# Delta recurrence: the output's state products right behind the w products, its attention products behind the state products

## The chip, the core and the metric

The kernel runs on one core of one Trainium2 chip. The metric is the device time in microseconds (us) of one execution; lower is better. Three executions of the kernel before took 5368.41, 5379.1 and 5381.07 us; their median, 5379.1, is the time that a changed kernel is compared with.

## The reference

The program is one inference step of a two-layer hybrid decoder (1024 prompt tokens and 8 sample tokens), in fp32. Only one of its stages is touched here: the chunked gated delta rule of the second layer, for the prompt. Its 8 heads have keys and values of 128 columns. Time is cut into chunks of C = 64 tokens, and a state `s` (128x128 for each head) is carried from chunk to chunk:

```python
def step(s, inp):
    q_i, k_i, u_i, w_i, g_i, a_i = inp
    v_new = u_i - jnp.einsum('bhck,bhkv->bhcv', w_i, s)
    o = (jnp.einsum('bhck,bhkv->bhcv', q_i * jnp.exp(g_i)[..., None], s)
         + jnp.einsum('bhij,bhjv->bhiv', a_i, v_new))
    g_last = g_i[..., -1:]
    s = (s * jnp.exp(g_last)[..., None]
         + jnp.einsum('bhck,bhcv->bhkv', k_i * jnp.exp(g_last - g_i)[..., None], v_new))
    return s, o
```

So `v_new` needs the old state, the new state needs `v_new`, and the output `o` is a sum of two products: one of the old state (the state part) and one of `v_new` (the attention part). Nothing in the recurrence needs `o`.

## The kernel before

The program is a row of stages, each a block of its own with one instruction list for each engine. `delta_phase` is the stage of the recurrence. It loops over NPAIR = 8 pairs of chunks. For each pair it first prepares both chunks at once (norms, gates, Gram products, and five levels of a triangular solve, whose result is `xt`), and then takes the two chunks, p = 0 and p = 1, one after the other through the recurrence, since the second needs the first one's state. This last part is the one that is changed. The eight heads are one instruction each on TensorE, and one instruction for all heads on the other engines. For each chunk, in the order in which the parts depend on each other:

- **w products** (line 2129): TensorE, keys (`kbe`) times state `st_`, into banks 0 and 1.
- **r0** (line 2244): VectorE, `bv` minus the w products. TensorE waits for it (`r_ready`).
- **u products** (line 2134): TensorE, `xt` times r0, into banks 2 and 3.
- **vn** (line 2177): ScalarE copies them to `vn`, the new values. TensorE waits for it (`u_copied`). VectorE meanwhile scales the old state into `tmp` (line 2249).
- **state products** (line 2139): TensorE, `ktm` times `vn`, into banks 6 and 7.
- **output products** (lines 2141 and 2143): TensorE, for each head the state part (`st_` times `qe`) and then the attention part (`vn` times `at`), which accumulate in banks 4 and 5.
- **S** (line 2252): VectorE, `tmp` plus the state products, is the new state. It waits for `s_done`, which the last output product raises. TensorE's next w products wait for S (`s_ready`).

After p = 1, ScalarE copies the output of both chunks out of PSUM (line 2180, which also waits for `s_done`) and the norm of the output follows. An fp32 matmul of the program is two records in the trace, so eight heads are 16. The order of work on each engine is the order of the code; waits on semaphores are the only other rule. The profile shows `r0` as `dn_r`, `at` as `dn_mat`, `st_` as `dn_S` and `xt` as `dn_mxt`, and PSUM as `ps`.

Of the kernel before, what the change touches and what calls it, by code (L numbers as in the profile page):

```python
# [42 lines left out]
C = 64  # L43
# [1986 lines left out]
def delta_phase(T, ba):  # L2030
# [4 lines left out]
    nc, h, ps, io = T.nc, T.h, T.ps, T.io  # L2035
    sems = Sems(nc, "dn")
    S = {n: sems(n) for n in (
        "rows_in", "z_in", "squared", "sq_sum", "rn_log", "rn", "ba_cut", "spread", "l_copied", "l_exp", "unit", "turned", "k_copied",
        "ba_turned", "tm_ready", "kd_ready", "diff", "diff_exp", "keyed", "gram", "blocks_copied", "blocks_ready", "xm_ready", "xt_ready", "zt_done",
        "y_done", "y_ready", "z_done", "solved", "masked", "w_done", "r_ready", "u_done", "u_copied", "s_done", "s_ready",  # L2040
        "o_copied", "o_sq", "o_sum", "rs_log", "rs", "out_ready", "step", "cleared", "pe_passed", "end_diff", "end_exp",
        "state_out")}
    ones, ident, sel = T.const("ones"), T.const("ident"), T.const("sel")
    W = 2 * C
    with ExitStack() as ctx:
# [4 lines left out]
        Lb, eL, kb, kbe, qe, ktm, bv, r0, vn, st_, tmp, o, rs = (sb("_" + n, [P, 8, W]) for n in  # L2050
                                                              "Lb eL kb kbe qe ktm bv r0 vn S tmp o rs".split())
# [6 lines left out]
        bank = lambda b, hd: b + hd // 4  # L2058
        col = lambda hd, a=0, n=W: slice((hd % 4) * W + a, (hd % 4) * W + a + n)
# [27 lines left out]
        @block.tensor  # L2087
        def _(pe):
            with pe.Fori(0, NPAIR) as i:
                pe.wait_ge(S["squared"], i + 1)  # L2090
                for b in range(4):
                    mm = pe.matmul(ps[:, b, :], ones, qk[:, 4 * b:4 * b + 4, :], start=True, stop=True)
                mm.then_inc(S["sq_sum"], 1)
                pe.wait_ge(S["ba_cut"], i + 1)
                for b, r in ((4, slice(A_ROW, A_ROW + 8)), (6, slice(BETA_ROW, BETA_ROW + 8))):
                    for hd in range(8):
                        mm = pe.matmul(ps[:, bank(b, hd), col(hd)], sel[r, hd * P:(hd + 1) * P], bs[r, :], start=True, stop=True)
                mm.then_inc(S["spread"], 1)
                pe.wait_ge(S["unit"], i + 1)
                for b, src in ((0, qk[:, 8:16, :]), (2, X[:, 16:24, :])):  # L2100
                    for hd in range(8):
                        mm = pe.transpose(ps[:, bank(b, hd), col(hd)], src[:, hd, :], ident)
                pe.wait_ge(S["l_copied"], i + 1)
                mm = pe.transpose(ps[:, 4, 0:P], bs[:, :], ident)
                mm.then_inc(S["turned"], 1)
                pe.wait_ge(S["keyed"], i + 1)

                def gram(b, left, right):
                    for hd in range(8):
                        for p in range(2):  # L2110
                            c = slice(C * p, C * p + C)
                            mm = pe.matmul(ps[64 * p:64 * p + 64, b, hc(hd)], left(hd)[:, c], right(hd)[:, c], start=True,
                                           stop=True)
                    mm.then_inc(S["gram"], 1)

                k_, q_, kb_ = (lambda hd: qk[:, 8 + hd, :]), (lambda hd: qk[:, hd, :]), (lambda hd: kb[:, hd, :])
                gram(5, k_, kb_)
                gram(6, kb_, k_)
                gram(7, k_, q_)
                pe.wait_ge(S["tm_ready"], i + 1)  # L2120
                solve_levels_pe(pe, T, S, i, mtl, xm, xt, y, (0, 1, 2), S["pe_passed"])
                pe.wait_ge(S["masked"], i + 1)
                pe.wait_ge(S["solved"], i + 1)
                for p in range(2):
                    r, a = slice(64 * p, 64 * p + 64), C * p
                    c = slice(a, a + C)
                    pe.wait_ge(S["s_ready"], 2 * i + p + 1)
                    for hd in range(8):
                        mm = pe.matmul(ps[r, bank(0, hd), col(hd)], kbe[:, hd, c], st_[:, hd, :], start=True, stop=True)
                    mm.then_inc(S["w_done"], 1)  # L2130
                    pe.wait_ge(S["r_ready"], 2 * i + p + 1)
                    alone(pe, S["pe_passed"])
                    for hd in range(8):
                        mm = pe.matmul(ps[r, bank(2, hd), col(hd)], xt[r, hc(hd)], r0[r, hd, :], start=True, stop=True)
                    mm.then_inc(S["u_done"], 1)
                    pe.wait_ge(S["u_copied"], 2 * i + p + 1)
                    alone(pe, S["pe_passed"])
                    for hd in range(8):
                        pe.matmul(ps[:, bank(6, hd), col(hd)], ktm[r, hd, :], vn[r, hd, :], start=True, stop=True)
                    for hd in range(8):  # L2140
                        pe.matmul(ps[:, bank(4, hd), col(hd, a, C)], st_[:, hd, :], qe[:, hd, c], start=True, stop=False,
                                  skip_group_check=True)
                        mm = pe.matmul(ps[:, bank(4, hd), col(hd, a, C)], vn[r, hd, :], at[r, hc(hd)], start=False, stop=True,
                                       skip_group_check=True)
                    mm.then_inc(S["s_done"], 1)
                pe.wait_ge(S["o_sq"], i + 1)
                for b in range(2):
                    mm = pe.matmul(ps[:, b, :], ones, rs[:, 4 * b:4 * b + 4, :], start=True, stop=True)
                mm.then_inc(S["o_sum"], 1)

        @block.scalar
        def _(act):
            act.preload_act_table_set(EXP_LN_SET)
            with act.Fori(0, NPAIR) as i:
                act.wait_ge(S["rows_in"], 16 * i + 16)
                act.activation(qk[:, :, :], X[:, 0:16, :], ACT.Square).then_inc(S["squared"], 1)
                act.wait_ge(S["sq_sum"], i + 1)
                act.activation(qk[:, :, :], ps[:, 0:4, :].rearrange("p b (h w) -> p (b h) w", h=4), ACT.Ln,
                               bias=T.vec("eps_rms")).then_inc(S["rn_log"], 1)
                act.wait_ge(S["rn_log"], i + 1)  # L2160
                act.activation(qk[:, :, :], qk[:, :, :], ACT.Exp, scale=-0.5).then_inc(S["rn"], 1)
                act.wait_ge(S["spread"], i + 1)
                act.activation(Lb[:, :, :], two(4), ACT.Copy).then_inc(S["l_copied"], 1)
                act.wait_ge(S["l_copied"], i + 1)
                act.activation(eL[:, :, :], Lb[:, :, :], ACT.Exp).then_inc(S["l_exp"], 1)
                act.wait_ge(S["turned"], i + 1)
                act.activation(bt[:, :], ps[:, 4, 0:P], ACT.Copy).then_inc(S["ba_turned"], 1)
                act.wait_ge(S["end_diff"], i + 1)
                act.activation(ek[:, :], ek[:, :], ACT.Exp).then_inc(S["end_exp"], 1)
                act.wait_ge(S["diff"], i + 1)  # L2170
                act.activation(dt_[:, :], dt_[:, :], ACT.Exp)
                act.activation(dn[:, :], dn[:, :], ACT.Exp).then_inc(S["diff_exp"], 1)
                solve_levels_act(act, T, S, i, y, (0, 1, 2))
                for p in range(2):
                    r = slice(64 * p, 64 * p + 64)
                    act.wait_ge(S["u_done"], 2 * i + p + 1)
                    act.activation(vn[r, :, :], ps[r, 2:4, :].rearrange("p b (h w) -> p (b h) w", h=4), ACT.Copy)\
                       .then_inc(S["u_copied"], 1)
                act.wait_ge(S["s_done"], 2 * i + 2)
                act.activation(o[:, :, :], two(4), ACT.Copy).then_inc(S["o_copied"], 1)  # L2180
                act.wait_ge(S["o_copied"], i + 1)
                act.activation(rs[:, :, :], o[:, :, :], ACT.Square).then_inc(S["o_sq"], 1)
                act.wait_ge(S["o_sum"], i + 1)
                act.activation(rs[:, :, :], two(0), ACT.Ln, scale=1.0 / P, bias=T.vec("eps_rms")).then_inc(S["rs_log"], 1)
                act.wait_ge(S["rs_log"], i + 1)
                act.activation(rs[:, :, :], rs[:, :, :], ACT.Exp, scale=-0.5).then_inc(S["rs"], 1)
# [351 lines left out]
```

## Time and profile before

| what | us |
|---|---|
| median of three runs | 5379.1 |
| lowest and highest of them | 5368.41, 5381.07 |
| span of the profiled execution | 5365.0 |
| TensorE busy in that span | 4202.5 (78%) |
| VectorE busy | 2662.5 (50%) |
| ScalarE busy | 1202.0 (22%) |
| stretch of the delta stage, from its first to its last pair (3433.2 to 4300.4) | 867.2 |

The span runs from the first to the last instruction of the profiled execution, which has no time of its own listed beside it; the median of the runs is 14.1 us above the span. Busy shares are averages over stages with different limits, so the table says little of the delta stage; that one is read from its own rows further down. PE in the profile is TensorE's matmuls, PEld its weight loads, DVE is VectorE, ACT is ScalarE, POOL is GpSimd and SP is SyncE.

### The profile page before, as it was taken

Reading aid. Unit: us, or ns where it says so; the run is one execution under the profiler, and the core shown is the slowest. Engines: PE = TensorE matmul, PEld = TensorE weight load, DVE = VectorE, ACT = ScalarE, POOL = GpSimd, SP = SyncE. Lnnn points to the kernel's source line nnn. Section 1 sums busy time; section 2 is a strip of 40 time slices with the busy share of each in tenths; the row PEclk is TensorE's granted clock in tenths of the full one; section 3 lists DMA queues with packets and bytes.
Section 4 is the critical chain, followed back from the end, with each engine's and each line's share of the span. In section 5 each row is a group of like instructions: output and inputs, shape, how many; then the busy total and the mean of one; then the engine's idle time right before and its main releaser. Section 6 shows DMA issues by size and latency. Waiting matters only on the chain. (4 is left out here: it accounts for less than half of the span.)

```text
span 5365.0 us, 83010 instructions
## 1 busy us (share of the span) xinstructions
PE 4202.5 (78%) x29517; PEld 3455.9 (64%) x29517; DVE 2662.5 (50%) x3402; ACT 1202.0 (22%) x1838; POOL 244.3 (5%) x302
## 2 busy tenths in 40 slices
PE   7786876777766756999998799677767717999998
PEld 6684323333333336999998688565556607999998
DVE  2167877888888532344433444433333352344433
ACT  3213531111111112222232222211211111222232
POOL 0000000000000000000000000100010000000000
PEclk8898987788877768999999899866666659999999
DMA  2242046677776513111154122200000022111154
GB/s 93 89 142 91 12 150 208 227 246 247 239 242 221 169 55 118 40 48 48 67 160 158 64 88 80 64 17 17 26 24 17 5 90 107 56 44 44 56 160 138
DMA packets 273719, 558.51 MB, mean 104 GB/s; under 512 B 35889, under 2 KB 93617, under 8 KB 266906
## 3 DMA queue, kind: packets, MB, share of 16 engines
q1 hardware_dynamic: 167434, 367.46, 21.4%
q10 hardware_dynamic: 90000, 141.65, 8.1%
q0 software_dynamic: 16032, 45.92, 2.1%
q8 instruction: 171, 2.80, 0.2%
q14 instruction: 82, 0.67, 0.0%
HBM read 500.74 MB, written 54.56 MB: 104 GB/s over the span
## 5 line engine op out<-in xcount | busy, mean ns | idle before, releaser
L260 PE MATMUL ps<-ffn_hh,up_wh 128*128 128x344 f32 x2112 | 677.9, 321 | 60.1 <-DVE up_wl L252 60.1
L262 PE MATMUL ps<-ffn_hl,up_wh 128*128 128x344 f32 x2112 | 676.2, 320 | 0.0
L261 PE MATMUL ps<-ffn_hh,up_wl 128*128 128x344 f32 x2112 | 675.6, 320 | 0.0
L1045 PE MATMUL ps<-pg_v,pg_w 128*8 128x512 f32 x1024 | 370.7, 724 | 128.1 <-DMA pg_v<-in_v_pages 100.4
L260 PEld LDWEIGHTS ps<-ffn_hh,up_wh 128*128 128x128 f32 x2112 | 398.2, 189 | 61.2 <-issue 61.2
L261 PEld LDWEIGHTS ps<-ffn_hh,up_wl 128*128 128x128 f32 x2112 | 398.2, 189 | 0.0
L262 PEld LDWEIGHTS ps<-ffn_hl,up_wh 128*128 128x128 f32 x2112 | 398.1, 188 | 0.0
L450 PE MATMUL ps<-down_ah,down_wh 128*128 128x344 f32 x1056 | 345.8, 327 | 52.5 <-DVE down_al L482 31.3
L1106 DVE TENSOR_TENSOR pg_prod<-pg_k,pg_q 128x1024 f32<-128x1024 f32 x256 | 316.0, 1235 | 48.0 <-DVE rw_mxt L1417 14.5
L451 PE MATMUL ps<-down_ah,down_wl 128*128 128x344 f32 x1056 | 339.0, 321 | 0.0
L452 PE MATMUL ps<-down_al,down_wh 128*128 128x344 f32 x1056 | 338.9, 321 | 0.0
L1110 DVE TENSOR_REDUCE pg_z<-pg_prod 128x16 f32<-128x1024 f32 (+1 forms) x256 | 312.7, 1221 | 11.4 <-DVE pg_prod L1106 0.2
L252 DVE TENSOR_TENSOR down_wl<-down_w,down_wh 128x1408 fp32r<-128x1408 f32 x96 | 155.9, 1624 | 312.6 <-ACT down_wh L247 312.6
L260 PE MATMUL ps<-hh,odd_wh 128*128 128x344 f32 x792 | 257.9, 326 | 64.5 <-DVE odd_wl L252 64.5
L1045 PEld LDWEIGHTS ps<-pg_v,pg_w 128*8 128x8 f32 x1024 | 43.2, 101 | 344.8 <-DMA pg_v<-in_v_pages 287.5
L262 PE MATMUL ps<-hl,odd_wh 128*128 128x344 f32 x792 | 254.4, 321 | 0.0
L261 PE MATMUL ps<-hh,odd_wl 128*128 128x344 f32 x792 | 254.4, 321 | 0.0
L450 PEld LDWEIGHTS ps<-down_ah,down_wh 128*128 128x128 f32 x1056 | 199.6, 189 | 66.9 <-issue 52.5
L247 ACT ACTIVATE down_wh<-down_w 128x1408 fp32r<-128x1408 f32 x96 | 132.3, 1379 | 368.6 <-PE ps L452 341.2
L451 PEld LDWEIGHTS ps<-down_ah,down_wl 128*128 128x128 f32 x1056 | 200.8, 190 | 0.0
L452 PEld LDWEIGHTS ps<-down_al,down_wh 128*128 128x128 f32 x1056 | 199.9, 189 | 0.0
L260 PEld LDWEIGHTS ps<-hh,odd_wh 128*128 128x128 f32 x792 | 150.1, 190 | 73.4 <-ACT odd_row L1954 43.4
(427 smaller groups left out, 7812.4 us busy)
## 6 DMA issues: line engine op xcount, KB each, us to landing
pg_k<-in_k_pages SPq DMA_DIRECT2D x512, 256.0 KB, 4.4
pg_v<-in_v_pages ACTq DMA_DIRECT2D x512, 256.0 KB, 4.6
down_w<-in_w_down SPq DMA_DIRECT2D x96, 704.0 KB, 4.2
up_w<-in_w_ff SPq DMA_DIRECT2D x44, 1034.0 KB, 4.8
odd_w<-in_w_odd SPq DMA_DIRECT2D x33, 526.0 KB, 4.0
scratch_odd_rows<-odd_cv POOLq DMA_DIRECT2D x32, 516.0 KB, 4.5
dn_x<-scratch_odd_rows SPq DMA_DIRECT2D x8, 1536.0 KB, 7.9
scratch_x<-out_x POOLq DMA_DIRECT2D x16, 516.0 KB, 2.9
```

Source lines behind the costliest of these rows:

```text
L247: act.activation(hi, w, ACT.Copy).then_inc(rounded, 1)
L252: dve.tensor_tensor(lo, w, hi.bitcast(F32), ALU.subtract).then_inc(rest_ready, 1)
L260: pe.matmul(out, wh, xh, start=(k == 0), stop=False)
L261: pe.matmul(out, wl, xh, start=False, stop=False)
L262: mm = pe.matmul(out, wh, xl, start=False, stop=(k == n - 1))
L450: pe.matmul(ps[:, j, 0:GC], wh[:, v, wk], ah[:, kk, :], start=(kk == 0), stop=False)
L451: pe.matmul(ps[:, j, 0:GC], wl[:, v, wk], ah[:, kk, :], start=False, stop=False)
L452: mm = pe.matmul(ps[:, j, 0:GC], wh[:, v, wk], al[:, kk, :], start=False, stop=(kk == FT - 1))
L1045: pe.matmul(self.T.ps[c:c + H_A, 7, :], wts[:, :, g], self.vp[:, n, :], start=(g < 4), stop=(g >= NPG - 4), tile_position=(0, c), skip_gro ...
L1106: dve.tensor_tensor(self.prod[:, :, :], self.kp[:, n:n + 2, :], self.q[:, :].unsqueeze(1).to_broadcast([P, 2, D_A]), ALU.mult).then_inc(se ...
L1110: dve.tensor_reduce(z.rearrange("p h n -> p n h"), self.prod[:, :, :].rearrange("p n (h d) -> p n h d", h=H_A), AX.X, ALU.add).then_inc(se ...
```

## The change

The eight state parts of the output move up: they are issued right behind the w products, ahead of TensorE's wait for r0. The eight attention parts stay behind the state products, now without the state parts in between. `s_done` is raised by the last state product, ahead of the attention parts, and a new signal `o_done`, raised by the last attention part, is what ScalarE's copy of the output waits for. Since a start flag clears the accumulation marks of a whole PSUM bank, only the first head of each bank has it now.

```diff
                     mm.then_inc(S["w_done"], 1)
+                    for hd in range(8):
+                        pe.matmul(ps[:, bank(4, hd), col(hd, a, C)], st_[:, hd, :], qe[:, hd, c], start=(hd % 4 == 0), stop=False,
+                                  skip_group_check=True)
                     pe.wait_ge(S["r_ready"], 2 * i + p + 1)
...
                     for hd in range(8):
-                        pe.matmul(ps[:, bank(6, hd), col(hd)], ktm[r, hd, :], vn[r, hd, :], start=True, stop=True)
+                        mm = pe.matmul(ps[:, bank(6, hd), col(hd)], ktm[r, hd, :], vn[r, hd, :], start=True, stop=True)
+                    mm.then_inc(S["s_done"], 1)
                     for hd in range(8):
-                        pe.matmul(ps[:, bank(4, hd), col(hd, a, C)], st_[:, hd, :], qe[:, hd, c], start=True, stop=False,
-                                  skip_group_check=True)
                         mm = pe.matmul(ps[:, bank(4, hd), col(hd, a, C)], vn[r, hd, :], at[r, hc(hd)], start=False, stop=True,
                                        skip_group_check=True)
-                    mm.then_inc(S["s_done"], 1)
+                    mm.then_inc(S["o_done"], 1)
...
-                act.wait_ge(S["s_done"], 2 * i + 2)
+                act.wait_ge(S["o_done"], 2 * i + 2)
                 act.activation(o[:, :, :], two(4), ACT.Copy).then_inc(S["o_copied"], 1)
```

On TensorE, the chunk p = 0 of a pair stood like this before (one row for each matmul of the code, an equal run of them as one row with its count):

```order
 L2129 MATMUL ps<-dn_S,dn_kbe 64x128 x8
-L2134 MATMUL ps<-dn_r,dn_mxt 64x128 x8
-L2139 MATMUL ps<-dn_vn,dn_ktm 128x128 x8
-L2141 MATMUL ps<-dn_qe,dn_S 128x64
-L2143 MATMUL ps<-dn_mat,dn_vn 128x64
```

The last two rows repeat until there are eight of each. With the change the same chunk on the same engine, down to the w products of p = 1, stands like this (line numbers are up to three higher):

```order
+L2132 MATMUL ps<-dn_qe,dn_S 128x64 x8
+L2137 MATMUL ps<-dn_r,dn_mxt 64x128 x8
+L2142 MATMUL ps<-dn_vn,dn_ktm 128x128 x8
+L2145 MATMUL ps<-dn_mat,dn_vn 128x64 x8
 L2127 REGISTER_ALU
 L2129 MATMUL ps<-dn_S,dn_kbe 64x128 x8
```

The state parts moved from behind the state products to ahead of the u products, and sixteen alternating rows became two runs of eight. VectorE, ScalarE, GpSimd and SyncE keep every instruction in its place; only what ScalarE's copy of the output waits for is another semaphore, and VectorE's S finds `s_done` raised by an earlier instruction. No DMA is added, removed or moved.

## Rows read from the trace of the kernel before

**Rows 1.** Busy time by stretch: the delta stage, all engines (PEclk: granted TensorE clock)

```profile
3433.20:4300.40 867.20, 612.10 (x6118) 507.56 (x6119) 293.24 (x309) 147.11 (x158) 63.46 (x40) 0.66 0.07 19
```

**Rows 2.** Timeline where the delta stage ends and the next one begins

```profile
4306.13 1.23 DVE L2258 TENSOR_TENSOR h<-dn_o,dn_z 128x1024 f32 x1 [0.22 <-DVE dn_o L2255]
4308.61 0.39 SPq L2290 DMA_DIRECT2D ds_x<-scratch_odd_rows  x1
4312.56 0.31 ACT L2333 ACTIVATE ds_sq<-ds_x 128x128 f32<-128x128 f32 x1 [2.65 <-DMA ds_x<-scratch_odd_rows]
```

**Rows 3.** Groups by line, PE, 3420 to 4300: busy, mean ns | idle before, releaser

```profile
L2141 PE MATMUL ps<-dn_qe,dn_S 128*128 128x64 f32 x256 | 87.9, 447 | 0.0
L2143 PE MATMUL ps<-dn_mat,dn_vn 64*128 64x64 f32 x256 | 87.8, 445 | 0.0
L2139 PE MATMUL ps<-dn_vn,dn_ktm 64*128 64x128 f32 x256 | 60.0, 425 | 19.2 <-ACT dn_vn L2177 19.2
...
L2129 PE MATMUL ps<-dn_S,dn_kbe 128*64 128x128 f32 x256 | 44.9, 349 | 19.8 <-DVEq L2253 11.6 <-DVEq L1418 8.3
L2134 PE MATMUL ps<-dn_r,dn_mxt 64*64 64x128 f32 x256 | 43.5, 338 | 23.4 <-DVEq L2246 23.4
```

**Rows 4.** Timeline, one pair's two chunks: start, us, engine, line [idle before <-releaser]

```profile
3705.41 1.96 PE L2129 MATMUL ps<-dn_S,dn_kbe 128*64 128x128 f32 x16 [1.03 <-DVEq L1418]
3707.40 1.21 DVE L2244 TENSOR_TENSOR dn_r<-dn_bv,ps 64x1024 f32<-64x1024 f32 x1 [2.30 <-PE ps L2129]
...
3708.82 1.93 PE L2134 MATMUL ps<-dn_r,dn_mxt 64*64 64x128 f32 x16 [1.45 <-DVEq L2246]
3710.78 1.02 ACT L2177 ACTIVATE dn_vn<-ps 64x1024 f32<-64x1024 f32 x1 [7.70 <-PE ps L2134]
3711.83 1.22 DVE L2249 TENSOR_TENSOR dn_tmp<-dn_S,dn_eL 128x1024 f32<-128x1024 f32 x1 [3.22 <-ACT dn_vn L2177]
3711.92 3.48 PEld L2139 LDWEIGHTS ps<-dn_vn,dn_ktm 64*128 64x128 f32 x16 [1.41 <-issue]
3711.95 3.75 PE L2139 MATMUL ps<-dn_vn,dn_ktm 64*128 64x128 f32 x16 [1.20 <-ACT dn_vn L2177]
3715.62 0.69 PE L2141 MATMUL ps<-dn_qe,dn_S 128*128 128x64 f32 x2
3716.24 0.69 PE L2143 MATMUL ps<-dn_mat,dn_vn 64*128 64x64 f32 x2
...
3724.87 0.69 PE L2143 MATMUL ps<-dn_mat,dn_vn 64*128 64x64 f32 x2
3725.67 1.22 DVE L2252 TENSOR_TENSOR dn_S<-dn_tmp,ps 128x1024 f32<-128x1024 f32 x1 [12.62 <-PE ps L2143]
3727.01 3.68 PE L2129 MATMUL ps<-dn_S,dn_kbe 128*64 128x128 f32 x16 [1.45 <-DVEq L2253]
...
3732.15 3.64 PE L2134 MATMUL ps<-dn_r,dn_mxt 64*64 64x128 f32 x16 [1.47 <-DVEq L2246]
...
3736.99 3.75 PE L2139 MATMUL ps<-dn_vn,dn_ktm 64*128 64x128 f32 x16 [1.20 <-ACT dn_vn L2177]
...
3750.64 1.02 ACT L2180 ACTIVATE dn_o<-ps 128x1024 f32<-128x1024 f32 x1 [13.80 <-PE ps L2143]
```

**Rows 5.** Timeline: a run of eight in another stage, 128-column weights, 2 moving columns

```profile
870.91 1.71 PE L1052 MATMUL ps<-consts,pg_fold 128*128 128x2 f32 x8
```

**Rows 6.** Busy time by stretch, same pair: solve, w, u, state and output products

```profile
3682.20:3690.40 8.20, 7.32 (x128) 7.04 (x128) 2.80 (x3) 0.60 (x1) 1.02 (x1) 0.50 0.01 2
3690.40:3705.40 15.00, 10.87 (x322) 10.08 (x320) 4.81 (x7) 2.39 (x4) 0.00 (x0) 0.98 0.01 2
3705.40:3707.40 2.00, 1.96 (x16) 1.72 (x16) 0.00 (x0) 0.00 (x0) 0.00 (x0) 1.00 0.00 0
3708.80:3710.80 2.00, 1.93 (x16) 1.71 (x16) 0.00 (x0) 0.01 (x1) 0.00 (x0) 1.00 0.00 0
3711.90:3715.60 3.70, 3.65 (x16) 3.48 (x16) 1.16 (x1) 0.00 (x0) 0.00 (x0) 0.50 0.02 4
3715.60:3725.60 10.00, 9.96 (x33) 7.98 (x32) 0.00 (x0) 0.00 (x0) 0.00 (x0) 0.50 0.00 0
3727.00:3730.70 3.70, 3.68 (x16) 3.28 (x16) 0.00 (x0) 0.00 (x0) 0.00 (x0) 0.50 0.00 0
```

**Rows 7.** Busy time by stretch, first pair: w of p = 1, and what follows it

```profile
3509.90:3513.40 3.50, 3.20 (x15) 3.20 (x16) 0.19 (x1) 0.00 (x0) 0.00 (x0) 0.50 0.00 0
3513.40:3516.70 3.30, 1.83 (x17) 1.62 (x16) 1.22 (x1) 0.00 (x0) 0.00 (x0) 1.00 0.00 0
```

**Rows 8.** Timeline, PE: the first products of solve levels one to four

```profile
3682.30 1.97 PE L1377 MATMUL ps<-dn_mxm,dn_mtl 64*64 64x64 f32 x32 [11.51 <-DVEq L2236]
...
3688.49 1.95 PE L1377 MATMUL ps<-dn_mxm,dn_mtl 64*64 64x64 f32 x32
...
3693.30 1.15 PE L1377 MATMUL ps<-dn_mxm,dn_mtl 64*64 64x64 f32 x32
...
3697.30 1.15 PE L1377 MATMUL ps<-dn_mxm,dn_mtl 64*64 64x64 f32 x32
```

More of the change, by code:

```diff
@@ L2040, in delta_phase @@
         "y_done", "y_ready", "z_done", "solved", "masked", "w_done", "r_ready", "u_done", "u_copied", "s_done", "s_ready",
-        "o_copied", "o_sq", "o_sum", "rs_log", "rs", "out_ready", "step", "cleared", "pe_passed", "end_diff", "end_exp",
+        "o_done", "o_copied", "o_sq", "o_sum", "rs_log", "rs", "out_ready", "step", "cleared", "pe_passed", "end_diff", "end_exp",
         "state_out")}
```

## The prediction

> **What bounds the kernel now.** I first looked for how the delta stage joins the rest. It takes 867.2 us of the 5365.0 of the span [rows 1]. It ends with VectorE's last product at 4306.13, and the next stage's first DMA is issued only at 4308.61, with ScalarE waiting for it [rows 2]. So nothing of the next stage runs under this one, and what the stage loses or gains the program loses or gains.
>
> Then the groups by line, for the stage's TensorE alone [rows 3]. The two output products are its costliest groups, 87.9 and 87.8 us, and TensorE never waits ahead of them. Ahead of the u products it sits idle for 23.4 us, waiting for VectorE's r0 (16 times, 1.46 each), and ahead of the w products for 11.6 us, waiting for S (8 times, 1.45 each).
>
> Then the timeline of one pair, where the chain can be followed step by step [rows 4]. From the w products of p = 0 at 3705.41 to those of p = 1 at 3727.01 it is 21.60 us; from there to the copy of the output at 3750.64 it is 23.63. TensorE is in this chain all the time but for three pauses: r0, vn and S. The reader is to see that S (3725.67) starts only when the last output product is done, though what it needs, the state products, was there at about 3715.6; the output products, 9.94 us from 3715.62 to 3725.56, stand in the way of the chain.
>
> Last, the granted clock [rows 6]. TensorE has two levels, 1.2 and 2.4 GHz (0.5 and 1.0 in the rows). In this pair the solve begins at the low level and ends at the high one, w and u of p = 0 run at the high one (1.96 and 1.93 us for 16 instructions), and all that follows at the low one (3.68, 3.64 and 3.75 for 16) [rows 4, 6].
>
> **The change, part by part.**
>
> *The wait for r0 is covered.* Behind the w products stand now 16 instructions of state part. VectorE's r0 takes 1.21 us and the whole pause is 1.45; the run that covers it lasts at least 1.95 (below). So the u products find r0 ready. If the cover were gone, 1.45 us for each chunk would come back.
>
> *The wait for S is covered, for p = 0.* `s_done` comes 16 instructions earlier; S (1.22 us, pause 1.45) and its input `tmp`, which is done at 3713.05 while the state products run to 3715.6, lie beside the attention parts. What is queued behind S on VectorE is r0 of p = 1, which waits for the w products anyway. For p = 1 nothing on the path waited for S, and ScalarE's copy of the output waits for the same last instruction as before, so its new signal costs nothing. Pauses removed: 2 x 1.45 + 1.45 = 4.35 us for a pair.
>
> *Two alternating groups become two runs.* The 32 output instructions of a chunk take 9.94 us today, 0.31 each. No row shows such a run of them alone, so I bound it. The nearest rows are runs of one form at the low level: 8 instructions with the same 128 columns of weights and 2 moving columns in 1.71 us, 0.214 each [rows 5], and the state products with 128 moving columns, 16 in 3.67 from start to next start, 0.23 each [rows 4]. The output products have 64 moving columns, between the two, so I take 16 in 3.65 us, which as a whole duration also holds the end of the run and the turn to the next form. At the high level I take 1.95, as w and u show. The upper bound is today's 4.97 for 16, no gain from grouping.
>
> The weight rows bear on this: while the state products run (3.75 us), their weight loads are busy 3.48 us, all on the same 64 rows [rows 4], so loads go on beside matmuls on the same rows. The Trainium skill ("TensorE: Matmul & The Clock Gate", Part 3, The mechanism) says that a weight load overlaps matmuls in flight only when its row group differs; by that a run of one form would have its loads bare and grouping would bring nothing. This trace disagrees with it for the state products. By the rule the gain would be the third rival's.
>
> *Sum with the clock levels as they are now.* For p = 0: w 1.96, state part 1.95, u 1.93, pause for vn 1.20, state products 3.67, attention part 3.65: 14.36 us against 21.60. For p = 1, all low: 3.68 + 3.65 + 3.64 + 1.20 + 3.67 + 3.65 = 19.49 against 23.63. Saved: 7.24 + 4.14 = 11.38 for a pair, 91 us for eight.
>
> *The clock.* What it grants then no row shows outright. For it to rise: the w products of p = 1 in the first pair ran at the low level, and the stretch behind them had the high one [rows 7]; the solve climbs in the same way after some 8 us of work [rows 6]. Against it: the output products today keep TensorE busy 9.96 of 10.00 us and stay low [rows 6], and w of p = 1 in the shown pair brings nothing either. After the change state products, attention part, w, state part and u follow one another with no pause at all, and w is the run that lifted it in the first pair. I take it that the clock is back behind w of p = 1: its state part and u then take 1.95 + 1.93 instead of 3.65 + 3.64, 3.41 us for a pair. And in p = 0 one of the two pauses that lie ahead of the fall is gone; I take half of what state products and attention part would gain at the high level: (3.67 + 3.65 - 2 x 1.95) / 2 = 1.71. Both ends are kept: nothing of this (91 us), and both chunks at the high level throughout, 45.23 - 2 x 10.94 = 23.35 for a pair, 187 us for eight.
>
> *Sum.* 11.38 + 3.41 + 1.71 = 16.50 us for a pair, 132 for eight. Against the profiled span that is 5365.0 - 132 = 5233; the median of the runs lies 14.1 above the span, so 5379.1 - 132 = 5247 us.
>
> **The rivals.**
>
> 1. *The clock does not come back.* The runs are as short as taken, but each stays at its present level: 91 us, 5288. For it: half of a chunk's work still uses 64 rows or moves 64 columns, and the busy 10 us at the low level [rows 6]. Against it: [rows 7].
>
> 2. *All of both chunks at the high level.* 187 us, 5192. Against it: the pause for vn stays, and behind it today's clock is low [rows 4, 6].
>
> 3. *Grouping brings nothing*, because loads and matmuls of one form follow one another instead of overlapping: 4.35 us of pauses for a pair, 35 us, 5344. For it: within one head, two instructions of one form already stand together today, and the pair still costs 0.62 [rows 4]. Against it: [rows 4, 5].
>
> 4. *The clock is lost in the solve.* Slower, as one mechanism: with other times in the tail, the next pair's solve meets the clock at another moment. Today the solve's first level and about half of its second run low, and a level takes 6.19 us low and 4.00 high [rows 8]. If all of it stayed low, 3.5 levels would cost 7.7 us, and w, u and the state part of p = 0 another 1.72 + 1.71 + 1.70: 12.8 for a pair against 11.38 saved, 11 us slower, 5390. It decides only from 11.4 us on, that is if the clock stays low through the whole solve and into w. Against it: ahead of the solve TensorE is idle for 11.51 us [rows 8], before and after alike, so the solve starts low either way, and its own products are unchanged.
>
> That a wait is dropped and nothing gained is excluded by the rows: the pauses are on the chain, and the covering work is TensorE's own and has to be done anyway.
>
> **How the numbers follow.** Forecast (paces as taken, the clock partly back) 0.60; rival 1, 0.20; rival 2, 0.05; rival 3, 0.10; rival 4, 0.03; nothing at all, 0.02. The predicted time is that of the forecast, 5247 us. The range leaves out no more than 2 in 10: down to three quarters of the way from 132 to 187 us saved (174, 5205), and up to midway between rivals 1 and 3 (63 saved, 5316, say 5317). A measurement of this kernel can tell about 0.3%, 16 us, from no change. All of the forecast and rivals 1 to 3 are faster by more than that; with some room for a smaller rival 3, faster 0.93, within 0.3% 0.04, slower 0.03.
>
> **What the profile after would show.** The idle ahead of the u products and the w products of p = 1 gone from the groups by line (23.4 and 11.6 us today); the pause for vn still 1.20. A state part of 16 instructions in 1.95 or 3.65 us and an attention part likewise, told apart by the granted clock of their stretch; 4.97 would mean rival 3. From w of p = 0 to w of p = 1 about 12.6 to 14.4 us, from there to the copy of the output about 16. S ends before the attention part does. The solve as today, 23 us from its first product to the w products. The prediction is wrong if runs of one form cost 0.31 us an instruction, or if the clock's moments move through the whole pair, so that the preparation, untouched by the code, takes another time.

## The result, and the profile after

The changed kernel takes 5223.94 us (median of four runs, 5219.92 to 5236.87) beside 5373.76 us (5362.74 to 5381.07) for the kernel before in the same comparison: the ratio is 0.9729, with a 95% interval from 0.9715 to 0.9743. 5247 was forecast, with a range from 5205 to 5317.

The groups by line of the stage, changed kernel, for TensorE (busy, mean ns of one | idle before, releaser), answer to [rows 3]:

```profile
L2145 PE MATMUL ps<-dn_mat,dn_vn 64*128 64x64 f32 x256 | 52.8, 392 | 0.0
...
L2129 PE MATMUL ps<-dn_S,dn_kbe 128*64 128x128 f32 x256 | 43.4, 341 | 8.3 <-DVEq L1418 8.3
...
L2142 PE MATMUL ps<-dn_vn,dn_ktm 64*128 64x128 f32 x256 | 36.1, 297 | 19.2 <-ACT dn_vn L2179 19.2
L2132 PE MATMUL ps<-dn_qe,dn_S 128*128 128x64 f32 x256 | 33.6, 286 | 0.0
L2137 PE MATMUL ps<-dn_r,dn_mxt 64*64 64x128 f32 x256 | 31.3, 272 | 0.0
```

The idle ahead of the u products (23.4 us before) and that ahead of the w products for S (11.6) are gone; the pause for vn is what it was, 19.2. The two output groups fell from 87.9 and 87.8 us to 33.6 and 52.8.

One pair of the changed kernel, as a timeline, answers to [rows 4]:

```profile
3585.27 1.96 PE L2129 MATMUL ps<-dn_S,dn_kbe 128*64 128x128 f32 x16 [1.03 <-DVEq L1418]
3587.15 1.86 PEld L2132 LDWEIGHTS ps<-dn_qe,dn_S 128*128 128x128 f32 x16 [0.17 <-issue]
3587.15 2.00 PE L2132 MATMUL ps<-dn_qe,dn_S 128*128 128x64 f32 x16
3587.26 1.21 DVE L2246 TENSOR_TENSOR dn_r<-dn_bv,ps 64x1024 f32<-64x1024 f32 x1 [2.30 <-PE ps L2129]
3589.08 1.96 PE L2137 MATMUL ps<-dn_r,dn_mxt 64*64 64x128 f32 x16
...
3592.24 2.34 PE L2142 MATMUL ps<-dn_vn,dn_ktm 64*128 64x128 f32 x16 [1.20 <-ACT dn_vn L2179]
...
3594.38 3.51 PE L2145 MATMUL ps<-dn_mat,dn_vn 64*128 64x64 f32 x16
3594.69 1.22 DVE L2254 TENSOR_TENSOR dn_S<-dn_tmp,ps 128x1024 f32<-128x1024 f32 x1 [1.34 <-PE ps L2142]
3597.82 3.31 PE L2129 MATMUL ps<-dn_S,dn_kbe 128*64 128x128 f32 x16
...
3601.05 2.00 PE L2132 MATMUL ps<-dn_qe,dn_S 128*128 128x64 f32 x16
...
3602.98 1.96 PE L2137 MATMUL ps<-dn_r,dn_mxt 64*64 64x128 f32 x16
...
3606.14 2.57 PE L2142 MATMUL ps<-dn_vn,dn_ktm 64*128 64x128 f32 x16 [1.20 <-ACT dn_vn L2179]
...
3608.50 3.51 PE L2145 MATMUL ps<-dn_mat,dn_vn 64*128 64x64 f32 x16
...
3612.05 1.02 ACT L2182 ACTIVATE dn_o<-ps 128x1024 f32<-128x1024 f32 x1 [6.06 <-PE ps L2145]
```

From w to w it is 12.55 us (21.60 before), from there to the copy of the output 14.23 (23.63). S is done at 3595.91, two microseconds before the end of the attention part that covers it (3597.89).

The granted clock of the same pair, by stretch (last columns: PEclk, DMA share, GB/s): w and state part of p = 0, state products, attention part, w of p = 1, and its state part with u:

```profile
3585.20:3589.00 3.80, 3.73 (x32) 3.57 (x32) 1.21 (x1) 0.00 (x0) 0.00 (x0) 1.00 0.00 0
...
3592.20:3594.10 1.90, 1.86 (x15) 1.89 (x16) 1.15 (x1) 0.00 (x0) 0.00 (x0) 0.92 0.04 9
3594.40:3597.80 3.40, 3.40 (x17) 3.30 (x16) 1.22 (x1) 0.00 (x0) 0.00 (x0) 0.50 0.00 0
3597.90:3600.60 2.70, 2.70 (x13) 2.70 (x14) 0.00 (x0) 0.00 (x0) 0.00 (x0) 0.50 0.00 0
3601.00:3605.00 4.00, 3.94 (x34) 3.58 (x32) 1.22 (x1) 0.03 (x1) 0.00 (x0) 1.00 0.00 0
```

The level falls in the state products, and is back at the end of w of p = 1. Only every second pair looks like this. In the other four the level falls a little later, in the attention part, and comes back in the state part of p = 1; such a pair takes 25.9 us from w to the copy of the output, the shown kind 26.8:

```profile
3683.51 2.02 PE L2142 MATMUL ps<-dn_vn,dn_ktm 64*128 64x128 f32 x16 [1.20 <-ACT dn_vn L2179]
3685.37 2.98 PE L2145 MATMUL ps<-dn_mat,dn_vn 64*128 64x64 f32 x16
```

Across kernels I compare the stage itself, from the first pair's first operation to the last copy of an output. In the changed kernel its two ends are these rows, 716.1 us apart:

```profile
3438.83 1.91 ACT L2158 ACTIVATE dn_qk<-dn_x 128x2048 f32<-128x2048 f32 x1 [6.89 <-DMA dn_x<-scratch_odd_rows]
...
4154.94 1.02 ACT L2182 ACTIVATE dn_o<-ps 128x1024 f32<-128x1024 f32 x1 [6.14 <-PE ps L2145]
```

Worked out in the same way it was 863.5 us before, so the stage gave 147.4 of the 149.8 us between the medians. In the profiles of this study what lies ahead of the stage took between 3433.3 and 3452.9 us, and what lies behind it between 1068.2 and 1070.4. So differences of medians under some 10 us say little; the stage says more, though each stage time comes from one profiled execution. Each ratio is to the kernel before in its own comparison, where its median lay between 5370.6 and 5373.9.

| kernel | median us | ratio to before, 95% interval | stage us |
|---|---|---|---|
| before | 5373.76 | | 863.5 |
| changed | 5223.94 | 0.9729 [0.9715, 0.9743] | 716.1 |
| grouped in place | 5323.02 | 0.9901 [0.9884, 0.9919] | 809.9 |
| groups of two | 5351.0 | 0.9951 [0.9932, 0.9969] | 840.1 |
| late signal | 5244.3 | 0.9757 [0.9737, 0.9777] | 729.2 |
| state part behind u | 5280.23 | 0.9832 [0.9808, 0.9856] | 770.7 |
| state part split | 5196.85 | 0.9667 [0.9651, 0.9682] | 688.3 |
| filler behind u | 5190.08 | 0.9653 [0.9637, 0.967] | 675.3 |
| split and filler | 5181.54 | 0.965 [0.9636, 0.9663] | 673.3 |
| filler ahead of the solve, six | 5235.67 | 0.9745 [0.9732, 0.9758] | 718.0 |
| the same, nine | 5217.88 | 0.9708 [0.9692, 0.9723] | 709.9 |
| all fillers and the split | 5165.52 | 0.9607 [0.9591, 0.9623] | 648.3 |

### The profile page after: what moved, and what is told of

Same layout as the page of the kernel before. It is cut to its first block and busy times, and to the rows that moved or that the text cites. A ratio compares the mean times of both kernels' runs of the same rounds, so it can differ in the third digit from the quotient of the medians.

```text
span 5223.3 us, 83010 instructions
## 1 busy us (share of the span) xinstructions
PE 4090.6 (78%) x29517; PEld 3380.3 (65%) x29517; DVE 2662.9 (51%) x3402; ACT 1202.3 (23%) x1838; POOL 244.2 (5%) x302
```

## The experiments

The theory: the gain has three parts, the two pauses that are covered, the runs of one form that replace the alternation, and a granted clock that is high more often. Matmuls of one form have the same rows and columns (the state part has 128 rows, the attention part 64), and a turn is the change from one form to the next. The chief rival is the third of the prediction, that grouping brings nothing. Diffs are against the changed kernel.

**Grouped in place.**

The state parts go back behind the state products, and one signal stands behind the attention parts, for both waits.

```diff
-                    for hd in range(8):
-                        pe.matmul(ps[:, bank(4, hd), col(hd, a, C)], st_[:, hd, :], qe[:, hd, c], start=(hd % 4 == 0), stop=False,
-                                  skip_group_check=True)
                     pe.wait_ge(S["r_ready"], 2 * i + p + 1)
...
-                    mm.then_inc(S["s_done"], 1)
+                    for hd in range(8):
+                        pe.matmul(ps[:, bank(4, hd), col(hd, a, C)], st_[:, hd, :], qe[:, hd, c], start=(hd % 4 == 0), stop=False,
+                                  skip_group_check=True)
                     for hd in range(8):
...
-                    mm.then_inc(S["o_done"], 1)
+                    mm.then_inc(S["s_done"], 1)
...
```

> Only the grouping: state parts and attention parts as two runs of eight, both where the alternating pairs stood, one signal behind the last of them as before; the pauses for r0 and for S come back. My account (a run of one form goes at 0.21 us an instruction at the low clock level where alternating ones take 0.31): the output products take about 7.2 us for a chunk instead of 9.94, 42 us in all against the kernel before, about 5330. The rival (loads and matmuls of one form follow one another, so grouping brings nothing): the time of the kernel before, 5374.

Its timeline from state products of p = 0 to u of p = 1:

```profile
3917.10 3.75 PE L2139 MATMUL ps<-dn_vn,dn_ktm 64*128 64x128 f32 x16 [1.20 <-ACT dn_vn L2178]
3920.78 3.67 PE L2141 MATMUL ps<-dn_qe,dn_S 128*128 128x64 f32 x16
3924.39 3.67 PE L2144 MATMUL ps<-dn_mat,dn_vn 64*128 64x64 f32 x16
3929.51 3.46 PE L2129 MATMUL ps<-dn_S,dn_kbe 128*64 128x128 f32 x16 [1.45 <-DVEq L2254]
3934.43 2.13 PE L2134 MATMUL ps<-dn_r,dn_mxt 64*64 64x128 f32 x16 [1.47 <-DVEq L2247]
```

The output products take 7.28 us (3920.78 to 3928.06) instead of 9.94, at the same low level: 2.66 for a chunk, 43 us for sixteen. The rival falls. The stage gained 53.6; the rest is in the main u of p = 1, which now finds the high level (2.13 us instead of 3.64, 12 us for eight pairs).

**Groups of two heads.**

As the kernel grouped in place, but with state and attention parts of two heads at a time:

```diff
+                    for g in range(0, 8, 2):
+                        for hd in (g, g + 1):
+                            pe.matmul(ps[:, bank(4, hd), col(hd, a, C)], st_[:, hd, :], qe[:, hd, c], start=(hd % 4 == 0),
...
+                        for hd in (g, g + 1):
+                            mm = pe.matmul(ps[:, bank(4, hd), col(hd, a, C)], vn[r, hd, :], at[r, hc(hd)], start=False, stop=True,
...
```

> A smaller dose: the output products in the old place in groups of two heads (two state parts, two attention parts, and so on), so half as many turns from one form to the other; signal and pauses as in the kernel before. If each turn costs a fixed time (0.27 + 0.35 us for two instructions today against 0.21 each inside a run), a chunk saves 8 x 0.19 = 1.5 us: about 25 us against the kernel before, 5349. If what costs is the form of the instructions and not the turns: 5374.

```profile
3940.96 1.11 PE L2142 MATMUL ps<-dn_qe,dn_S 128*128 128x64 f32 x4
3942.01 1.11 PE L2145 MATMUL ps<-dn_mat,dn_vn 64*128 64x64 f32 x4
3943.05 1.11 PE L2142 MATMUL ps<-dn_qe,dn_S 128*128 128x64 f32 x4
```

In this timeline a group of four instructions takes 1.04 us from start to start; a group of two took 0.62 [rows 4], one of sixteen 3.61 (above). That is 0.19 us for each turn and 0.213 for each instruction, all three, at the low level. The stage gained 23.4 us where 25 was expected. That the two parts of a head accumulate in the same place could be the reason instead of the turn; the split and filler kernel below speaks against it.

**Late signal.**

The signal for S goes back behind the attention parts, and the copy of the output waits for it too.

```diff
-                    mm.then_inc(S["s_done"], 1)
...
-                    mm.then_inc(S["o_done"], 1)
+                    mm.then_inc(S["s_done"], 1)
...
```

> The change without its new signal: state parts ahead of the u products, attention parts as one run, but the new state waits for the last attention part as before. Undoes the cover of S alone. At unchanged clock levels the pause of 1.45 us comes back once in a pair: 12 us above the changed kernel, about 5236. If the unbroken stretch of state products, attention part and w products is also what brings the clock back in p = 1, state part and u of p = 1 fall to the low level (3.65 and 3.64 instead of 2.00 and 1.96), 27 us more: about 5262.

```profile
3880.24 3.67 PE L2129 MATMUL ps<-dn_S,dn_kbe 128*64 128x128 f32 x16 [1.45 <-DVEq L2254]
3883.84 2.49 PE L2132 MATMUL ps<-dn_qe,dn_S 128*128 128x64 f32 x16
3886.27 1.96 PE L2137 MATMUL ps<-dn_r,dn_mxt 64*64 64x128 f32 x16
```

The pause of 1.45 ahead of w is back in this timeline of p = 1, and the stage is 13.1 us longer than with the change (the medians differ by 20). The pause alone makes 12. State part and u of p = 1 stay near the high level although the stretch ahead of w is now broken, and so they do in all eight pairs. So the second half of the expectation falls: the level comes back without the unbroken stretch.

**State part behind the u products.**

The eight state parts stand behind the u products instead of ahead of them.

```diff
-                    for hd in range(8):
-                        pe.matmul(ps[:, bank(4, hd), col(hd, a, C)], st_[:, hd, :], qe[:, hd, c], start=(hd % 4 == 0), stop=False,
-                                  skip_group_check=True)
                     pe.wait_ge(S["r_ready"], 2 * i + p + 1)
...
                     mm.then_inc(S["u_done"], 1)
+                    for hd in range(8):
+                        pe.matmul(ps[:, bank(4, hd), col(hd, a, C)], st_[:, hd, :], qe[:, hd, c], start=(hd % 4 == 0), stop=False,
+                                  skip_group_check=True)
                     pe.wait_ge(S["u_copied"], 2 * i + p + 1)
```

> The state part as one run behind the u products, so that it covers the pause for vn (1.20 us) instead of that for r0 (1.45); signals as in the change. By pauses alone: 16 x 0.25 = 4 us above the changed kernel, about 5228. If the clock level depends on where the pause lies (the pause for r0 stands behind w alone, so the high level may be lost before u), state part and u run low in p = 0 or p = 1, 1.7 us each: up to 5280.

```profile
3881.27 1.96 PE L2129 MATMUL ps<-dn_S,dn_kbe 128*64 128x128 f32 x16 [1.03 <-DVEq L1418]
3884.68 1.96 PE L2134 MATMUL ps<-dn_r,dn_mxt 64*64 64x128 f32 x16 [1.45 <-DVEq L2248]
3886.57 3.67 PE L2137 MATMUL ps<-dn_qe,dn_S 128*128 128x64 f32 x16
3890.17 3.78 PE L2142 MATMUL ps<-dn_vn,dn_ktm 64*128 64x128 f32 x16
```

The timeline shows r0's 1.45 back and vn's 1.20 gone, a difference of 4 us, but the stage lost 54.6 against the change. u still runs high (1.96), but the state part behind it takes 3.67 instead of 2.00 and the state products 3.78 instead of 2.34: with the pause for r0 left and that for vn covered, the level falls by the state part of both chunks (in every second pair in the midst of it), and no longer only in the state products or the attention part. Which pause is covered matters by what happens to the clock (some 50 us) far more than by the pause's own length (4 us).

**State part split.**

```diff
-                    for hd in range(8):
+                    for hd in range(4):
...
                     mm.then_inc(S["u_done"], 1)
+                    for hd in range(4, 8):
+                        pe.matmul(ps[:, bank(4, hd), col(hd, a, C)], st_[:, hd, :], qe[:, hd, c], start=(hd % 4 == 0), stop=False,
...
```

> The state part in two halves: four heads ahead of the u products, four behind them, so that both pauses are partly covered; signals as in the change. 8 instructions take about 1.0 us at the high level, so of r0's 1.45 some 0.45 stays and of vn's 1.20 some 0.2: 0.55 us less pause for a chunk than the changed kernel, 9 us in all, less one more turn of form (0.15 each, 2 us): about 5217. If the pause for vn is what loses the clock in both chunks, state products, attention part and the w products of p = 1 run high more often, up to 30 us more: 5190. If the narrow forms lose it and not the pause: 5217 or above.

Its pairs take 83.4 to 93.5 us. A good and a bad pair, from the attention part of p = 0 on, in the timeline:

```profile
3850.77 1.89 PE L2148 MATMUL ps<-dn_mat,dn_vn 64*128 64x64 f32 x16
3852.59 1.96 PE L2129 MATMUL ps<-dn_S,dn_kbe 128*64 128x128 f32 x16
...
3757.79 2.64 PE L2148 MATMUL ps<-dn_mat,dn_vn 64*128 64x64 f32 x16
3760.36 3.67 PE L2129 MATMUL ps<-dn_S,dn_kbe 128*64 128x128 f32 x16
3763.96 1.97 PE L2132 MATMUL ps<-dn_qe,dn_S 128*128 128x64 f32 x8
3765.86 3.67 PE L2137 MATMUL ps<-dn_r,dn_mxt 64*64 64x128 f32 x16
```

In the good pair all of both chunks runs high, with 0.42 us left of the pause for r0 and 0.16 of that for vn, and so it is in five of the eight pairs. In the bad one the level falls in the attention part, and then a whole chunk without any idle stays low. There are two of this kind, and in one more the level falls there and is back by u of p = 1. The median fell by 27 us, more than the pauses explain (9) and less than the upper case.

**Filler behind the u products.** The output is that of the change; the eight added instructions' results are read by nobody.

```diff
                     mm.then_inc(S["u_done"], 1)
+                    for hd in range(4):
+                        pe.matmul(ps[r, bank(0, hd), col(hd)], kbe[:, hd, c], st_[:, hd, :], start=True, stop=True)
```

> The change, plus useless work: the w products of four heads are issued once more behind the u products, into the banks that nobody reads any more, so that TensorE works through the pause for vn (8 instructions, about 1.0 us of 1.20 at the high level). Output as before. If clock levels don't depend on that pause: same as the changed kernel, 5224, or some us above it. If the pause loses the high level: attention part and w products of p = 1, low today (3.51 and 3.31 us), come nearer to 1.95, and the kernel with more work is faster, by up to 2 us for each chunk, 32 us: down to 5192.

The busy time by stretch, over both chunks of a pair:

```profile
3845.00:3867.00 22.00, 21.02 (x176) 19.57 (x176) 7.33 (x6) 2.61 (x3) 0.00 (x0) 1.00 0.01 1
```

The timeline of the same pair, from the state products of p = 0 to w of p = 1:

```profile
3851.98 2.02 PE L2144 MATMUL ps<-dn_vn,dn_ktm 64*128 64x128 f32 x16 [0.18 <-ACT dn_vn L2181]
3853.84 1.89 PE L2147 MATMUL ps<-dn_mat,dn_vn 64*128 64x64 f32 x16
3855.66 1.96 PE L2129 MATMUL ps<-dn_S,dn_kbe 128*64 128x128 f32 x16
```

More work, and 34 us less time (stage 40.8 less): the clock is at 1.00 throughout both chunks of all eight pairs, attention part and w of p = 1 take 1.89 and 1.96 us instead of 3.51 and 3.31, and the pause is 0.18. The pause for vn is what cost the high level in the changed kernel. The filler adds work and not only fills the pause, but the split did the same in five pairs with what was left of the pauses and no work added.

**Split and filler.** The split, with two repeated heads of w products ahead of the u products (into bank 2) and one behind them (into bank 0).

> The state part in two halves as in the split kernel, and what is left of the two pauses filled with useless repeats of w products (two heads ahead of the u products, one head behind them). If the high level is lost only through what is left of the pauses, every pair takes what the undisturbed pairs of the split kernel take, 83.4 us and a little more, instead of 90.5: 57 us below the changed kernel, about 5170. If the split kernel's slow pairs (93.5 us) come from elsewhere, it stays near the split kernel, 5197, or above it for the added work.

The first half of the state part and the repeat behind it, in its timeline:

```profile
3920.13 1.10 PE L2132 MATMUL ps<-dn_qe,dn_S 128*128 128x64 f32 x8
3921.16 0.65 PE L2135 MATMUL ps<-dn_S,dn_kbe 128*64 128x128 f32 x4
```

All eight pairs of its trace take 21.11 us from w to the copy of the output, and 84.4 to 85.4 as a whole. So the bad pairs of the split do come from what was left of the pauses. 5170 was too low: a good pair of the split takes 20.56 from w to the copy, so the added work costs 0.55 a pair, and the rest of the difference lies ahead of w, where the clock's moments differ: 83.4 us was the best of the split's undisturbed pairs, the others took 84.1 to 84.5. The timeline also prices a turn at the high level: eight instructions of the state part take 1.03 us from start to start, and sixteen took 1.93 in the changed kernel (3587.15 to 3589.08), which makes 0.11 for each instruction and 0.13 for the turn; the split's expectation had 0.15. State part and repeat write different banks and the repeat continues no sum, so a turn costs without the accumulation.

**Filler ahead of the solve.** Useless work in an unused bank, six matmuls in one kernel and nine in the other; the output is that of the change.

```diff
                 pe.wait_ge(S["tm_ready"], i + 1)
+                for n in range(6):
+                    pe.matmul(ps[:, 3, :], ones, qk[:, 0:4, :], start=True, stop=True)
```

> The change, plus useless work in another place: six matmuls of 512 columns into an unused bank while TensorE waits about 11 us for the first solve level. Prices the low level in the solve alone. In the changed kernel the solve takes 22.9 us from its first product to the w products, of which nearly two levels are low; a high level takes 4.00 us, so all five high would take 20.1: 2.8 us for a pair, 22 us in all, about 5202. If the solve's pace is set by VectorE and ScalarE between its products and not by the clock: 5224. If the useless matmuls end too late they cost what they overrun.

> The change plus useless work ahead of the solve, as in the earlier filler there, but nine matmuls instead of six: the six took 5.42 us at the high level and left 3.82 us idle, in which the level was lost again before the first solve level ended. Nine end some 1.2 us before the solve. If the idle time is what loses the level, the solve starts high and takes about 20.1 us instead of 22.9: 22 us below the changed kernel, about 5202, as long as the chunks behind it keep their times. If the solve's narrow forms lose it by themselves: no gain, 5224 to 5240.

Busy time by stretch, with six, in one pair: filler, and the first 7.3 us of the solve:

```profile
3566.40:3571.90 5.50, 5.42 (x12) 2.20 (x12) 5.12 (x5) 0.00 (x0) 3.25 (x3) 1.00 0.20 58
3575.70:3583.00 7.30, 6.52 (x126) 6.36 (x128) 2.80 (x3) 0.60 (x1) 0.89 (x1) 0.54 0.01 2
```

With nine, the whole solve:

```profile
3569.40:3589.50 20.10, 15.20 (x448) 14.11 (x448) 7.61 (x10) 2.98 (x5) 0.92 (x1) 1.00 0.01 2
```

In this pair and four more, six end 3.8 us before the solve, the level is lost again as it begins (0.54), and it takes 22.6 us. In the other three they end 2.1 us before it, the low stretch is shorter, and it takes 21.3 to 21.4. But the chunks give that back (one pair takes 32.1 us from w to the copy), and nothing is gained: 718.0 us of stage. Nine end 1.26 us before it, and the solve takes 20.12 us in all eight pairs, as expected, instead of some 22.9. But the median came down by 6 us only and not 22: from w to the copy of the output it now takes 27.3 to 32.2 us instead of 25.9 to 26.9. The next stretch gave most of it back, since the level falls at another moment of the chunk.

**All fillers and the split.**

> The split state part with fillers in both pauses (5182 measured) and the nine matmuls ahead of the solve together. If the two gains are of different stretches and add up: 2.8 us less for a pair, about 5160. If the solve doesn't hold the level, or the chunks' times move with the moment at which the level changes: 5180 or above.

With both stretches held high the gains stay: every solve 20.12 us, every pair of chunks 21.11, the stage 648.3 us and the median 5165.52, the fastest kernel of the study. It is 58 us below the change and 208 below the kernel before, though it does more work. The first pair, from its solve to the copy of its output, as busy time by stretch:

```profile
3467.80:3509.10 41.30, 36.27 (x620) 33.36 (x620) 14.94 (x16) 5.05 (x8) 0.96 (x1) 1.00 0.01 2
```

An early `s_done` with the state parts left behind the state products wasn't tried: S would overwrite the state that they still read.

## Why the prediction was right

*The two pauses* went as told, to 0.0 in the groups by line: 35 us in all by the rows of before.

*The runs of one form* were taken at 3.65 us for 16 at the low level and 1.95 at the high one; measured 3.51 to 3.67, and 2.00. The rule of the Trainium skill ("TensorE: Matmul & The Clock Gate", Part 3, The mechanism), that a weight load overlaps matmuls in flight only when its row group differs, is not what happens here: the state part's loads, all on the same 128 rows, are busy 1.86 us while its matmuls are busy 2.00, both from 3587.15 on. By the rule grouping would have brought nothing; in the kernel grouped in place it brought 43 us. What the alternation cost is 0.19 us a turn.

*The clock* is the term that was mis-sized. In the forecast's 132 us, 35 are pauses, 42 are turns, and 55 are the clock: 3.41 and 1.71 us for a pair, and 1.70 for the state part of p = 0, which stands behind w at the high level. In the stage's 147.4 the pauses are the same 35 and the turns 43, so some 69 are left to the clock. In the shown pair the sum had 14.36 - 1.71 = 12.65 us for p = 0, and 12.55 was measured. For p = 1 it had 19.49 - 3.41 = 16.08, and 14.23 was measured: the state products, which I left wholly at the low level, ran mostly high (2.57 us, 2.36 to the next start, instead of 3.67), and w came out at 3.23 to the next start instead of 3.68. The other kind of pair lies further from the sum in p = 0 (11.7 to 11.8 us) and as far in p = 1 (14.2).

*The reason given for the clock* was partly wrong. That one pause less ahead of the fall keeps the level longer is borne out (filler behind u; state part behind u). That an unbroken stretch brings it back is not: it came back behind a pause with the late signal, and stayed away for a whole unbroken chunk in a bad pair of the split. So the 3.41 us for p = 1 came out as told for a reason that the runs do not bear out, and the half taken for p = 0 rested on no row; that both came so near is luck in part. What lifts the level at which moment stays open.

*Rival 4* (a solve that stays low) didn't occur: 22.8 to 23.2 us from the solve's first product to w, 22.6 to 23.1 before. Its price was about right in the other direction: by it one and a half levels less at the low clock are worth 3.3 us, and with the nine fillers five high levels saved 2.8 for a pair.

## What to carry to other kernels

Issue matmuls of one form together: two forms that alternate cost a fixed time for each turn, here 0.19 of every 0.62 us, nearly a third of the stretch. When work is moved to cover a wait on TensorE, look at the granted clock of what comes behind: a pause of 1.2 us that is left can cost more in the runs after it than in itself, and useless matmuls in it can pay. Judge such a gain by the whole loop, since the next stretch may give it back.

## What was not expected of the hardware

Adding eight useless instructions for each chunk made the kernel 34 us faster; splitting the state part and adding work in three pauses made it 58 us faster. In the changed kernel, with its pause of 1.20 us for vn, the level fell in the run behind that pause or in the next one, and with 0.18 us left of the pause it never fell. In the split, 0.42 and 0.16 us left of the two pauses were enough for a fall in three of eight pairs. Ahead of the solve, 3.8 us of idle behind 5.42 us of dense work at 1.00 lost the level.
